# A decoder layer in one kernel: the feed-forward loop's fourth weight group joins the seven-product scheme, one weight sum of each group is made by a DMA

## The chip, the cores and the metric

One core of one Trainium2 chip. The time is the device time of one execution in microseconds (us); the kernel before takes 2042.21 us (median of three runs, 2042.13 to 2042.24).

## What is computed

A hybrid decoder layer on 256 tokens, model width 2048, float32 in and out:

```python
x = x + 0.5 * swiglu(rmsnorm(x, ffn1_norm), ffn1_w_gate, ffn1_w_up, ffn1_w_down)
h = rmsnorm(x, mix_norm)
merged = (sigmoid(g_d + b_gate_dil) * (dilated_attention(...) @ w_proj_dil)
          + sigmoid(g_f + b_gate_fox) * (forgetting_attention(...) @ w_proj_fox))
x = x + merged @ w_out
x = x + 0.5 * swiglu(rmsnorm(x, ffn2_norm), ffn2_w_gate, ffn2_w_up, ffn2_w_down)
return rmsnorm(x, final_norm)
# swiglu(x, g, u, d) = (silu(x @ g) * (x @ u)) @ d;  D_FF = 5632
```

The change touches the two `swiglu` stages only.

## The kernel before, in words

**Split products.** A float32 matrix is split into a rounded part (`..._hi`, type fp32r, made by ACT with a copy) and the rest (`..._lo`, made by DVE as original minus rounded). A product is three matmuls: hi·hi, hi·lo, lo·hi. Weights come in *loads* of 1 MB (four row blocks of 128 by 512 columns, tile `raw`, four places) and are used in *slabs* of two row blocks (128x1024 elements in a place). A slab goes through three engines: ACT rounds it (`round_step`, into `w_hi` or `more_hi`), DVE makes its low part (`split_step`, into `w_lo` or `more_lo`), PE multiplies. The slabs have a ring of six places (`FFN_RING`): ACT may round slab m only when PE has finished slab m-6, and each engine works its slabs in order. `hi_ready`, `lo_ready` and `slab_done` count them.

**A step of the feed-forward loop** (`ffn`, lines 946 to 978 for PE) makes one chunk of 512 of the 5632 hidden columns; a first chunk is made outside the loop (`FIRST`, 16 slabs), then come 10 steps (`STEPS`) in each of the two feed-forward stages, 20 in all. A step has 33 slabs. The 2048 rows of the gate and up weights are four groups of 512. Groups 1, 2 and 3 go by a scheme of Strassen's kind (`paired`): two token tiles and the two weights gate and up make a 2x2 block product with seven products in place of eight. Each of the seven is one slab on one token operand, 6 matmuls of 128x512. Three of the seven weight operands are plain halves of a load, the other four are sums T1 to T4 that DVE makes first (`weight_sum`, four additions of 128x1024 to a group, into tile `sums`). Group 0 is done directly: four slabs of 12 matmuls. Eight *down* slabs of 12 matmuls each, for the product of the chunk before with the down weight, end the step. DVE also turns the seven results into gate and up (`partial`, `up_sums`, `chunk_buf`: adds out of PSUM), makes `hidden`, and the low part of its transpose (`hT_lo`, 128x512 twice).

**What sets the order.** Every engine's order is written out in loops over the slab number o. ACT and DVE run six slabs ahead of PE: at o they handle slab o+6. The DVE line that places the sums (L1781 to L1786) puts T1 ahead of the split of the slab of its group with number 1, T2 ahead of number 2, T4 ahead of number 4, while the products stand in the order T3, gate, T1, T2, up, T4, gate (`PRODUCTS`, L112): every sum has at least one other slab's split between itself and its own slab's split. DVE's sequence of adds at the end is L1937 to L1971. SP issues each load when `lo_ready` has reached the slab given by `FREE` (L120). Down results are copied by ACT to `gate_buf` and added to `xres` by accumulating DMAs that POOL issues, four to a step (L1729 to L1735).

## Time and profile before

| | |
|---|---|
| median of three runs | 2042.21 us |
| span of the profiled execution | 2040.2 us |
| PE busy | 2027.8 us (99%), 9204 matmuls |
| DVE busy | 1858.9 us (91%) |
| ACT busy | 1267.5 us (62%) |
| POOL busy | 87.6 us (4%) |
| DMA | 441 MB, mean 216 GB/s |

The profiled execution has no time of its own beside its span (first to last instruction); the three runs, which lie within 0.11 us of each other, take 2.0 us more than that span. The span has the first feed-forward stage up to about 675 us, the attention and merge stages, and the second feed-forward stage from about 1360 us. Busy times of successive instructions of one engine overlap a little, so what an instruction costs its engine is read as the distance from its start to the next start. In a row of a timeline, an instruction's start, its duration, engine and line come first, then what it writes and reads; idle time before it and who ended that stand in brackets.

### The profile page before, as it was taken

The page shows a single profiled execution, that of the slowest core. Times are in us where ns is not written, and L with a number is a line of the kernel's source. Part 1 is how long each engine was busy: PE and PEld are TensorE (multiplying, and loading weights), DVE is VectorE, ACT ScalarE, POOL GpSimd, SP SyncE. Part 2 cuts the span into 40 slices and gives each one's busy share as a digit, 9 for nine tenths or more (in the row PEclk, how much of TensorE's full clock was granted, in tenths as well). Part 3 has the DMA queues.
Part 4 walks back from the last instruction along what each step waited for, and adds up shares of the span by engine and source line. Part 5 has one row for each costly group of instructions (what it writes and reads, how often), then busy time and mean ns, then how long its engine had stood idle before and what let it go on. Part 6 is the DMA issues. An engine that isn't in the chain of part 4 may idle for free.

```text
span 2040.2 us, 26364 instructions
## 1 busy us (share of the span) xinstructions
PE 2027.8 (99%) x9204; PEld 1678.7 (82%) x9204; DVE 1858.9 (91%) x1897; ACT 1267.5 (62%) x1474; POOL 87.6 (4%) x80
## 2 busy tenths in 40 slices
PE   9999999999999999999999999999999999999998
PEld 7888888888888888888888888888888888888886
DVE  7999999999999798887689999799999999999997
...
GB/s 301 206 211 259 230 236 246 227 236 227 246 247 235 157 186 183 198 177 157 183 134 227 189 243 182 211 186 192 242 223 250 244 232 211 260 225 240 247 231 127
DMA packets 222143, 441.03 MB, mean 216 GB/s; under 512 B 7648, under 2 KB 7824, under 8 KB 221936
## 3 DMA queue, kind: packets, MB, share of 16 engines
...
q8 instruction: 47, 0.77, 0.1%
...
HBM read 400.13 MB, written 2.10 MB: 197 GB/s over the span
## 4 chain that ended last, share of the span: by engine, by line
PE 98%; DVE 1%; ACT 0%; DMA 0%; issue 0%; SPq 0%; ACTq 0%; DVEq 0%
PE ps L765 16%; PE ps L767 16%; PE ps L766 16%; PE ps L778 12%; PE ps L780 12%; PE ps L779 12%; PE ps L1002 2%; PE ps L1003 2%; PE ps L1001 2%; PE ps L1050 2%; PE ps L1052 2%; PE ps L1051 2%; PE ps L856 1%; PE ps L834 0%; DMA xres<-in_x 0%; PE ps L1169 0%
## 5 line engine op out<-in xcount | busy, mean ns | idle before, releaser
L1788 DVE TENSOR_TENSOR w_lo<-raw,w_hi 128x1024 fp32r<-128x1024 f32 x280 | 337.9, 1219 | 7.2 <-ACT w_hi L1356 4.9
L1356 ACT ACTIVATE w_hi<-raw 128x1024 fp32r<-128x1024 f32 x280 | 290.8, 1053 | 72.6 <-PE ps L767 54.0
L1356 ACT ACTIVATE w_hi<-sums 128x1024 fp32r<-128x1024 f32 x160 | 169.8, 1063 | 204.8 <-PE ps L767 71.4
L1788 DVE TENSOR_TENSOR w_lo<-sums,w_hi 128x1024 fp32r<-128x1024 f32 x160 | 195.3, 1222 | 33.8 <-ACT w_hi L1356 31.1
L765 PE MATMUL ps<-w_hi,hT_hi 128*128 128x512 f32 x536 | 208.8, 390 | 0.0
L767 PE MATMUL ps<-w_hi,hT_lo 128*128 128x512 f32 x536 | 208.5, 389 | 0.0
L766 PE MATMUL ps<-w_lo,hT_hi 128*128 128x512 f32 x536 | 208.5, 389 | 0.0
L1788 DVE TENSOR_TENSOR more_lo<-raw,more_hi 128x1024 fp32r<-128x1024 f32 x140 | 169.2, 1219 | 6.6 <-ACT more_hi L1356 5.6
L765 PE MATMUL ps<-w_hi,xT_hi 128*128 128x512 f32 x424 | 170.1, 401 | 0.0
L1356 ACT ACTIVATE more_hi<-raw 128x1024 fp32r<-128x1024 f32 x140 | 146.4, 1054 | 32.6 <-PE ps L767 23.8
L767 PE MATMUL ps<-w_hi,xT_lo 128*128 128x512 f32 x424 | 165.7, 391 | 0.0
L766 PE MATMUL ps<-w_lo,xT_hi 128*128 128x512 f32 x424 | 165.2, 390 | 0.0
L1734 POOL DMA_DIRECT2D xres<-gate_buf x72 | 84.9, 1179 | 1848.3 <-ACT gate_buf L1490 1803.3
L1356 ACT ACTIVATE more_hi<-sums 128x1024 fp32r<-128x1024 f32 x80 | 85.1, 1063 | 99.1 <-DVE sums L1770 24.1
L778 PE MATMUL ps<-w_hi,xT_hi 128*128 128x512 f32 x354 | 139.8, 395 | 0.0
L780 PE MATMUL ps<-w_hi,xT_lo 128*128 128x512 f32 x354 | 138.1, 390 | 0.0
L779 PE MATMUL ps<-w_lo,xT_hi 128*128 128x512 f32 x354 | 137.9, 390 | 0.0
L1675 ACT ACTIVATE w_hi<-raw 128x1024 fp32r<-128x1024 f32 x87 | 92.2, 1060 | 63.6 <-PE ps L767 51.8
L2128 DVE TENSOR_TENSOR w_lo<-raw,w_hi 128x1024 fp32r<-128x1024 f32 x85 | 102.2, 1220 | 20.2 <-ACT w_hi L1576 20.2
L1576 ACT ACTIVATE w_hi<-raw 128x1024 fp32r<-128x1024 f32 x85 | 89.1, 1057 | 47.2 <-PE ps L1052 31.0
L2317 DVE TENSOR_TENSOR w_lo<-raw,w_hi 128x1024 fp32r<-128x1024 f32 x87 | 104.8, 1220 | 14.9 <-ACT w_hi L1675 14.9
L767 PEld LDWEIGHTS ps<-w_hi,hT_lo 128*128 128x128 f32 x536 | 100.6, 188 | 20.9
...
## 6 DMA issues: line engine op xcount, KB each, us to landing
...
```

The lines of the kernel that those rows point to most:

```text
L765: nc.tensor.matmul(acc, hi, hi_w[:, j], start=first and j == 0, stop=False)
L766: nc.tensor.matmul(acc, hi, lo_w[:, j], start=False, stop=False)
L767: done = nc.tensor.matmul(acc, lo, hi_w[:, j], start=False, stop=last and j == 1)
L778: nc.tensor.matmul(acc, hi, hi_w[:, j], start=first and j == 0, stop=False)
L779: nc.tensor.matmul(acc, hi, lo_w[:, j], start=False, stop=False)
L780: done = nc.tensor.matmul(acc, lo, hi_w[:, j], start=False, stop=last and j == 1)
L1356: nc.scalar.activation(slot_hi(place, offset), src, ACT.Copy).then_inc(hi_ready, 1)
L1576: nc.scalar.activation(slot_hi(place, r), src, ACT.Copy).then_inc(hi_ready, 1)
L1675: nc.scalar.activation(slot_hi(place, offset), src, ACT.Copy).then_inc(hi_ready, 1)
L1788: nc.vector.tensor_tensor(slot_lo(place, offset), step_source(r)[0], slot_hi(place, offset).bitcast(F32), ALU.subtract).then_inc(lo_ready, 1)
L2128: nc.vector.tensor_tensor(slot_lo(place, r), dil_source(e)[0], slot_hi(place, r).bitcast(F32), ALU.subtract).then_inc(lo_ready, 1)
L2317: nc.vector.tensor_tensor(slot_lo(place, offset), merge_source(offset)[0], slot_hi(place, offset).bitcast(F32), ALU.subtract).then_inc(lo_ ...
```

## The change

Group 0 becomes a fourth group of seven products (now `PAIR_AT` = 0, 7, 14, 21; the direct slabs go), so a step has 36 slabs: 28 of 6 matmuls and 8 of 12. The signs are arranged so that all weight sums are additions. T1 is no longer made by DVE but by a DMA that POOL issues, which adds the gate load's half onto the up load's half in `raw` (`add_t1`, 512 KB); it waits for T3's sum (which reads the same half) and for the gate load. The seven products have the order T3, gate, T2, up, T1, T4, gate (`FFN_PRODUCTS`). DVE places T2 ahead of the split of number 2 of its group, T4 ahead of number 3, and T3 of the *next* group ahead of number 4. The eight down slabs' low parts are made in four pieces of 128x2048. The second up bank goes, so one combining add shrinks from 128x1024 to 128x512; the adds follow the splits at o = 23 to 28. The fourth group's sums of tokens are made once per stage (`sum_pairs`, `split_pairs` with `PAIR_FOURTH`) and kept in places of `xT_hi`, `xT_lo` that are no longer read. The loads come in the order of the groups.

```diff
-FIRST, STEP = 2 * WIDE, 33
+FIRST, STEP = 2 * WIDE, 36
...
-PAIR_AT, PAIR_GROUPS, PAIR_SLABS = (0, 7, 18), (1, 2, 3), 7
-PAIRS = len(PAIR_AT)
-DIRECT_AT, DIRECT_GROUP = 14, 0
+PAIR_AT, PAIR_GROUPS, PAIR_SLABS = (0, 7, 14, 21), (1, 2, 3, 0), 7
+PAIRS, PAIR_FOURTH = len(PAIR_AT), 3
...
+FFN_PRODUCTS = (("sum", T3), ("gate", 0), ("sum", T2), ("up", 1), ("sum", T1), ("sum", T4), ("gate", 1))
+FFN_SUMS = (T3, T2, T4)
+FFN_PLACE = {T3: 0, T2: 0, T4: 1}
+SUMS_STEP = len(FFN_SUMS) * PAIRS
 SUMS = SUMS_STEP * STEPS
 
-PAIR_LOADS, DIRECT_LOADS, DOWN_LOADS = ((0, 1), (2, 3), (6, 7)), (4, 5), 8
-
-FREE = (-6, -4, -2, 0, 5, 7, 12, 14, 16, 18, 23, 25)
+PAIR_LOADS, DOWN_LOADS = ((0, 1), (2, 3), (4, 5), (6, 7)), 8
+
+FREE = (-6, -4, -2, 0, 5, 7, 12, 14, 19, 21, 26, 28)
...
+    F_M1, F_M6, F_M7, F_TURN, F_GATE, F_UP0, F_M5 = 0, 1, 2, 3, 4, 6, 7
...
+                    if pair == PAIR_FOURTH:
+                        return lambda j: of_x(CT * s + 2 * j, 1)
                     return lambda j: (pair_hi[:, s, 2 * pair + j], pair_lo[:, s, 2 * pair + j])
 
                 for o, (bank, lhs) in enumerate((
-                        (M7, of_pair(S3)), (M1, of_tile(0, 0)), (M5, of_pair(S1)), (M6, of_pair(S2)),
-                        (UP0, of_pair(S4)), (GATE + 1, of_tile(1, 1)), (GATE, of_tile(1, 0)))):
+                        (F_M7, of_pair(S3)), (F_M1, of_tile(0, 0)), (F_M6, of_pair(S2)), (F_UP0, of_pair(S4)),
+                        (F_M5, of_pair(S1)), (F_GATE + 1, of_tile(1, 1)), (F_GATE, of_tile(1, 0)))):
...
-                    for o in range(2):
-                        slab(place, DIRECT_AT + o, (GATE, GATE + 1), of_x, CT * DIRECT_GROUP + 2 * o,
-                             False, False)
-                    pe.wait_ge(ht_lo, hid + TT)
-                    for o in range(2):
-                        direct_up(place, DIRECT_AT + 2 + o, CT * DIRECT_GROUP + 2 * o, o == 0, o == 1)
...
+                    pe.wait_ge(s_lo, (f + 1) * PAIRS)
+                    for o in paired(place, PAIR_FOURTH):
+                        pass
+                    pe.wait_ge(ht_lo, hid + TT)
                     for n in range(NN):
 
-                        pe.wait_ge(combined, merged + (1, 3, 4, 5)[n])
+                        pe.wait_ge(combined, merged + (1, 2, 4, 5)[n])
...
-            def round_step(place, offset, count):
+            def round_step(place, offset, count, added_before):
 
                 q, r = divmod(offset, STEP)
                 kind, pair, o = step_slab(r)
                 src, l = step_source(r)
-                if l is None:
-                    act.wait_ge(summed, count + SUMS_STEP * q + 4 * pair + PRODUCTS[o][1] + 1)
+                if l is not None:
+                    act.wait_ge(raw_landed[l % LOADS], place.landed(STEP_LOADS * q + l))
+                elif FFN_PRODUCTS[o][1] == T1:
+                    act.wait_ge(t1_added[pair], (added_before + q + 1) * 16)
                 else:
-                    act.wait_ge(raw_landed[l % LOADS], place.landed(STEP_LOADS * q + l))
+                    at = FFN_SUMS.index(FFN_PRODUCTS[o][1])
+                    act.wait_ge(summed, count + SUMS_STEP * q + len(FFN_SUMS) * pair + at + 1)
...
+                    if o == FIRST - 1:
+                        act.wait_ge(slab_done, first.slab(FIRST))
+                        round_pairs(f, PAIR_FOURTH)
...
+            def add_t1(f, q, pair):
+
+                up_l, gate_l = PAIR_LOADS[pair]
+                place = step_place(f, q)
+                pool.wait_ge(summed, f * SUMS + q * SUMS_STEP + len(FFN_SUMS) * pair + 1)
+                pool.wait_ge(raw_landed[gate_l % LOADS], place.landed(gate_l))
+                pool.dma_start(raw[:, up_l % LOADS, 0::2, :], raw[:, gate_l % LOADS, 0::2, :],
+                               accum_op=ALU.add).then_inc(t1_added[pair], 16)
+
...
+            for f in range(2):
+                add_t1(f, 0, 0)
+                add_t1(f, 0, 1)
+                for q in range(STEPS):
+                    add_t1(f, q, 2)
+                    add_t1(f, q, 3)
+                    if q < STEPS - 1:
+                        add_t1(f, q + 1, 0)
+                        for n in range(3):
+                            add_down(f, q, n)
+                        add_t1(f, q + 1, 1)
+                        add_down(f, q, 3)
...
-                done = count + SUMS_STEP * q + 4 * pair
-                out = sums[:, SUM_PLACE[which]]
+                done = count + SUMS_STEP * q + len(FFN_SUMS) * pair
+                out = sums[:, FFN_PLACE[which]]
                 if which == T3:
-                    dve.wait_ge(lo_ready, place.slab(base + at - 2))
+                    dve.wait_ge(summed, done)
                     dve.wait_ge(raw_landed[up_l % LOADS], place.landed(STEP_LOADS * q + up_l))
-                    made = nc.vector.tensor_tensor(out, up[:, 1::2, :], up[:, 0::2, :], ALU.subtract)
-                if which == T1:
-                    dve.wait_ge(lo_ready, place.slab(base + at - 1))
-                    dve.wait_ge(raw_landed[gate_l % LOADS], place.landed(STEP_LOADS * q + gate_l))
-                    made = nc.vector.tensor_tensor(out, up[:, 0::2, :], gate[:, 0::2, :], ALU.subtract)
+                    made = nc.vector.tensor_tensor(out, up[:, 1::2, :], up[:, 0::2, :], ALU.add)
                 if which == T2:
                     dve.wait_ge(lo_ready, place.slab(base + at + 1))
-                    dve.wait_ge(summed, done + T3 + 1)
-                    made = nc.vector.tensor_tensor(out, sums[:, SUM_PLACE[T3]], gate[:, 0::2, :], ALU.add)
+                    dve.wait_ge(raw_landed[gate_l % LOADS], place.landed(STEP_LOADS * q + gate_l))
+                    made = nc.vector.tensor_tensor(out, sums[:, FFN_PLACE[T3]], gate[:, 0::2, :], ALU.add)
                 if which == T4:
-                    dve.wait_ge(lo_ready, place.slab(base + at + 3))
-                    dve.wait_ge(summed, done + T2 + 1)
-                    made = nc.vector.tensor_tensor(out, gate[:, 1::2, :], sums[:, SUM_PLACE[T2]], ALU.subtract)
+                    dve.wait_ge(lo_ready, place.slab(base + at - 1))
+                    dve.wait_ge(summed, done + 2)
+                    made = nc.vector.tensor_tensor(out, gate[:, 1::2, :], sums[:, FFN_PLACE[T2]], ALU.add)
                 made.then_inc(summed, 1)
 
             def split_step(place, offset, count, final=False):
 
                 q, r = divmod(offset, STEP)
                 kind, pair, o = step_slab(r)
-                if kind == "paired" and o in (1, 2, 4):
-                    weight_sum(place, q, pair, {1: T1, 2: T2, 4: T4}[o], count)
-                if r + 1 in PAIR_AT:
-                    weight_sum(place, q, PAIR_AT.index(r + 1), T3, count)
-                if r == STEP - 1 and not final:
+                if kind == "paired" and o == 2:
+                    weight_sum(place, q, pair, T2, count)
+                if kind == "paired" and o == 3:
+                    weight_sum(place, q, pair, T4, count)
+                if kind == "paired" and o == 4 and pair + 1 < PAIRS:
+                    weight_sum(place, q, pair + 1, T3, count)
+                if r == STEP - 2 and not final:
                     weight_sum(place, q + 1, 0, T3, count)
+                if kind == "down" and o % 2 == 0:
+                    return
                 dve.wait_ge(hi_ready, place.slab(offset + 1))
+                if kind == "down":
+                    hi, lo = slots(place, offset - 1)
+                    nc.vector.tensor_tensor(lo, raw[:, step_source(r)[1] % LOADS], hi.bitcast(F32),
+                                            ALU.subtract).then_inc(lo_ready, 2)
+                    return
                 nc.vector.tensor_tensor(slot_lo(place, offset), step_source(r)[0],
                                         slot_hi(place, offset).bitcast(F32), ALU.subtract).then_inc(lo_ready, 1)
...
+                    if o == WIDE + 4:
+                        sum_pairs(f, PAIR_FOURTH)
+                    if o == FIRST - 1:
+                        split_pairs(f, PAIR_FOURTH)
...
-                        if o == 22:
-                            dve.wait_ge(slab_done, place.slab(22))
-                            dve.wait_ge(m1_copied, i + (f * STEPS + 1))
-                            nc.vector.tensor_tensor(u2, ps[:, M6], partial[:, PART_M1],
-                                                    ALU.add).then_inc(combined, 1)
-                        if last and o == 25:
+                        if last and o == 28:
                             gate_sum(place)
-                        if last and o == 26:
+                        if last and o == 29:
                             dve.wait_ge(combined, merged + 4)
-                            multiply_up([up_sums[:, 1 - t] for t in range(TT)], i * TT + (silu + TT))
+                            multiply_up([up_sums[:, 1 - t] for t in range(TT)], i * TT + (silu + TT), rstd_q)
                         if not last or o + FFN_RING < STEP:
                             split_step(place, o + FFN_RING, i * SUMS_STEP + count, last)
                         else:
                             split_slab(last_place(f), o + FFN_RING - STEP)
                         if o == 6:
-                            split_tokens(hid, 0, T)
-                        if o == 11:
-                            split_tokens(hid, 1, T)
-                        if o == 22:
+                            split_tokens(hid, 0, F_TURN)
+                        if o == 13:
+                            split_tokens(hid, 1, F_TURN)
+                        if o == 23:
+                            dve.wait_ge(slab_done, place.slab(24))
+                            dve.wait_ge(m1_copied, i + (f * STEPS + 1))
+                            nc.vector.tensor_tensor(u2, ps[:, F_M6], partial[:, PART_M1],
+                                                    ALU.add).then_inc(combined, 1)
+                        if o == 24:
                             dve.wait_ge(combined, merged + 1)
-                            nc.vector.tensor_tensor(u3, ps[:, M7], u2, ALU.add).then_inc(combined, 1)
-                        if o == 23:
+                            nc.vector.tensor_tensor(u3, ps[:, F_M7], u2, ALU.add).then_inc(combined, 1)
+                        if o == 25:
+                            dve.wait_ge(slab_done, place.slab(25))
                             dve.wait_ge(combined, merged + 2)
+                            nc.vector.tensor_tensor(u2, ps[:, F_UP0], u2, ALU.add).then_inc(combined, 1)
+                        if o == 26:
+                            dve.wait_ge(slab_done, place.slab(26))
+                            dve.wait_ge(combined, merged + 3)
                             nc.vector.tensor_tensor(up_sums[:, :, :],
-                                                    ps[:, M5:M5 + 1].broadcast_to([P, TT, CH]),
+                                                    ps[:, F_M5:F_M5 + 1].broadcast_to([P, TT, CH]),
                                                     partial[:, PART_U3:PART_U2 + 1], ALU.add)\
                               .then_inc(combined, 1)
...
-                        if not last and o == 26:
+                        if not last and o == 28:
                             gate_sum(place)
-                        if not last and o == 28:
+                        if not last and o == 31:
                             dve.wait_ge(combined, merged + 4)
-                            multiply_up([up_sums[:, 1 - t] for t in range(TT)], i * TT + (silu + TT))
+                            multiply_up([up_sums[:, 1 - t] for t in range(TT)], i * TT + (silu + TT), rstd_q)
```

DVE's rows of the second last step (written out behind the loop, so that nothing stands between the operations), kernel before: T1's sum (L1766), T2's (L1770) and T4's (L1774) of the third group; L1788 is the split into the low part.

```order
L1766 TENSOR_TENSOR sums<-raw 128x1024 [waits raw_landed3,lo_ready]
L1788 TENSOR_TENSOR more_lo<-raw,more_hi 128x1024 [waits hi_ready]
L1770 TENSOR_TENSOR sums<-sums,raw 128x1024 [waits summed,lo_ready]
L1788 TENSOR_TENSOR w_lo<-sums,w_hi 128x1024 [waits hi_ready] x2
L1774 TENSOR_TENSOR sums<-raw,sums 128x1024 [waits summed,lo_ready]
L1788 TENSOR_TENSOR w_lo<-raw,w_hi 128x1024 [waits hi_ready]
L1788 TENSOR_TENSOR w_lo<-sums,w_hi 128x1024 [waits hi_ready]
```

After the change, second group of the second last step: T3's split, then T2's sum (L1795), T4's (L1799), and T3's of the third group (L1791); L1822 is the split.

```order
L1822 TENSOR_TENSOR more_lo<-sums,more_hi 128x1024 [waits hi_ready]
L1822 TENSOR_TENSOR w_lo<-raw,w_hi 128x1024 [waits hi_ready]
L1795 TENSOR_TENSOR sums<-sums,raw 128x1024 [waits raw_landed3,lo_ready]
L1822 TENSOR_TENSOR w_lo<-sums,w_hi 128x1024 [waits hi_ready]
L1799 TENSOR_TENSOR sums<-raw,sums 128x1024 [waits summed,lo_ready]
L1822 TENSOR_TENSOR w_lo<-raw,w_hi 128x1024 [waits hi_ready]
L1791 TENSOR_TENSOR sums<-raw 128x1024 [waits raw_landed0,summed]
L1822 TENSOR_TENSOR w_lo<-raw,w_hi 128x1024 [waits hi_ready]
L1822 TENSOR_TENSOR more_lo<-sums,more_hi 128x1024 [waits hi_ready]
```

Before, T2's sum had the splits of T1 and T2 behind it (the row with x2); now T2's own split is the next operation.

DVE at the end of that step after the change, from the last paired slab: L1819 splits two down slabs at once, L2004 to L2016 are combining adds.

```order
L1822 TENSOR_TENSOR w_lo<-raw,w_hi 128x1024 [waits hi_ready]
L1819 TENSOR_TENSOR w_lo<-raw,w_hi 128x2048 [waits hi_ready]
L2004 TENSOR_TENSOR partial<-ps,partial 128x512 [waits m1_copied,slab_done]
L2008 TENSOR_TENSOR partial<-ps,partial 128x512 [waits combined]
L1819 TENSOR_TENSOR more_lo<-raw,more_hi 128x2048 [waits hi_ready]
L2012 TENSOR_TENSOR partial<-ps,partial 128x512 [waits combined,slab_done]
L2016 TENSOR_TENSOR up_sums<-ps,partial 128x1024 [waits combined,slab_done]
L1819 TENSOR_TENSOR w_lo<-raw,w_hi 128x2048 [waits hi_ready]
L1791 TENSOR_TENSOR sums<-raw 128x1024 [waits raw_landed0,summed]
```

PE's first down product waits (`combined`) for the add of L2004, which stands behind the piece that holds slabs 28 and 29.

POOL in the loop, after the change (before, L1734 four times a step alone):

```order
L1741 DMA raw<-raw 128x2x512 [waits raw_landed1,summed]
L1741 DMA raw<-raw 128x2x512 [waits raw_landed3,summed]
L1741 DMA raw<-raw 128x2x512 [waits raw_landed1,summed]
L1750 DMA xres<-gate_buf 128x2x512 [waits down_added0,down_copied]
L1750 DMA xres<-gate_buf 128x2x512 [waits down_added1,down_copied]
L1750 DMA xres<-gate_buf 128x2x512 [waits down_added2,down_copied]
L1741 DMA raw<-raw 128x2x512 [waits raw_landed3,summed]
L1750 DMA xres<-gate_buf 128x2x512 [waits down_added3,down_copied]
```

The four new DMAs (L1741) share POOL's queue with the four old ones (L1750), in this fixed order.

## Rows read from the trace of the kernel before

**Rows 1.** Page of the kernel before: span, engines' busy time, end chain by engine

```profile
span 2040.2 us, 26364 instructions
...
PE 2027.8 (99%) x9204; PEld 1678.7 (82%) x9204; DVE 1858.9 (91%) x1897; ACT 1267.5 (62%) x1474; POOL 87.6 (4%) x80
...
PE 98%; DVE 1%; ACT 0%; DMA 0%; issue 0%; SPq 0%; ACTq 0%; DVEq 0%
```

**Rows 2.** Windows: the start, one step of the first loop, one of the second

```profile
core 0: us, PE busy (x) PEld busy (x) DVE busy (x) ACT busy (x) POOL busy (x), PEclk, DMA share, GB/s
0.00:10.00 10.00, 6.39 (x36) 5.52 (x37) 3.07 (x6) 3.42 (x5) 0.20 (x4) 1.00 0.72 261
305.92:368.09 62.17, 62.17 (x280) 51.47 (x279) 59.14 (x55) 40.13 (x43) 4.71 (x4) 1.00 0.77 236
1600.00:1662.17 62.17, 62.17 (x280) 51.47 (x279) 59.14 (x55) 40.15 (x43) 4.71 (x4) 1.00 0.77 236
```

**Rows 3.** Timeline of PE: end of one step, the next one up to its transposes

```profile
start us, us, engine line op out<-in xcount [idle before <-releaser]
...
304.40 0.39 PE L767 MATMUL ps<-w_hi,hT_lo 128*128 128x512 f32 x1
304.63 0.39 PE L778 MATMUL ps<-more_hi,pair_hi 128*128 128x512 f32 x1
...
311.20 0.39 PE L780 MATMUL ps<-w_hi,pair_lo 128*128 128x512 f32 x1
```

**Rows 4.** Timeline of ACT: last down slabs, then the step's first roundings

```profile
304.83 1.06 ACT L1356 ACTIVATE w_hi<-sums 128x1024 fp32r<-128x1024 f32 x1 [1.66 <-PE ps L767]
305.80 1.01 ACT L1490 ACTIVATE gate_buf<-ps 128x1024 f32<-128x1024 f32 x1
306.70 1.05 ACT L1356 ACTIVATE more_hi<-raw 128x1024 fp32r<-128x1024 f32 x1
...
314.23 1.06 ACT L1356 ACTIVATE w_hi<-sums 128x1024 fp32r<-128x1024 f32 x1 [1.21 <-DVE sums L1770]
```

**Rows 5.** Timeline of DVE in the same stretch

```profile
305.92 1.23 DVE L1788 TENSOR_TENSOR w_lo<-sums,w_hi 128x1024 fp32r<-128x1024 f32 x1 [1.49 <-ACT w_hi L1356]
307.07 1.22 DVE L1762 TENSOR_TENSOR sums<-raw 128x1024 f32<-128x1024 f32 x1
...
312.90 1.22 DVE L1770 TENSOR_TENSOR sums<-sums,raw 128x1024 f32<-128x1024 f32 x1
314.04 2.52 DVE L1788 TENSOR_TENSOR w_lo<-sums,w_hi 128x1024 fp32r<-128x1024 f32 x2
316.47 1.22 DVE L1774 TENSOR_TENSOR sums<-raw,sums 128x1024 f32<-128x1024 f32 x1
```

**Rows 6.** Timeline of DVE between third product group and down slabs

```profile
343.46 0.69 DVE L1942 TENSOR_TENSOR partial<-ps,partial 128x512 f32<-128x512 f32 x1
344.06 1.22 DVE L1788 TENSOR_TENSOR w_lo<-raw,w_hi 128x1024 fp32r<-128x1024 f32 x1
345.20 0.68 DVE L1959 TENSOR_TENSOR partial<-ps,partial 128x512 f32<-128x512 f32 x1
...
358.45 1.41 DVE L1866 SCALAR_TENSOR_TENSOR hidden<-up_sums,rstd,chunk_buf 128x512 f32<-128x512 f32 x2
359.78 1.22 DVE L1770 TENSOR_TENSOR sums<-sums,raw 128x1024 f32<-128x1024 f32 x1
```

**Rows 7.** DMA queues in that step (kind: packets, MB, share of 16 engines)

```profile
q1 hardware_dynamic: 6336, 12.58, 56.8%
q0 software_dynamic: 1089, 2.10, 20.4%
```

**Rows 8.** Tile xres over the whole span: POOL issue, and landing of its DMAs

```profile
L1734 POOL DMA_DIRECT2D xres<-gate_buf x72: 1168/1179/1222, 104.4 to 1949.6; - x72
...
DMA to landing us min/median/max: 4.7/5.5/10.4
```

**Rows 9.** Timeline of POOL: one of the four issues of the step

```profile
307.10 1.18 POOL L1734 DMA_DIRECT2D xres<-gate_buf  x1 [4.25 <-ACT gate_buf L1490]
```

146 lines of the change are left out of this document (72 added, 74 removed).

## The prediction

> **What bounds the kernel now.** I read the page first, then one step of the loop by windows, then the timelines of PE, ACT and DVE at the same stretch, and last the DMA queues. The page says that PE is busy 99% of 2040.2 us and that 98% of the chain that ended last lies on it, with DVE at 91% [rows 1]. A step takes 62.17 us in both stages, PE busy all of it at a granted clock of 1.00 (the level of 2.4 GHz), DVE busy 59.14 [rows 2]. Matmuls follow each other at (311.20 - 304.63)/29 = 0.2266 us, though each lasts 0.39 [rows 3]; 270 of them are 61.2 us, so the eight transposes cost the other 0.96. PE is the bound, and DVE is close behind it. The reader should see how close. DVE's 128x1024 operations last 1.22 but start 1.14 apart (312.90 to 314.04, 344.06 to 345.20; the readings are rounded to 0.01, and I take 1.135), 128x512 ones 0.60 apart (343.46 to 344.06), the two that make `hidden` 1.33 together [rows 5, 6]. A step has 33 splits, 12 sums and 3 combining adds of 1024, and 4 operations of 512: 48 x 1.135 + 4 x 0.60 + 1.33 = 58.2 us of densely packed work in 62.17. The four microseconds left are waits for the ring of six, such as the 1.49 at 305.92, where DVE waits for ACT and ACT for PE [rows 4, 5].
>
> **The change, part by part.**
>
> PE: six matmuls fewer a step (264 for 270), 6 x 0.2266 = 1.36 us. Were PE still the bound, a step would take 60.81 and 20 steps would save 27 us.
>
> DVE's work: 28 splits, 12 sums and two adds of 1024 make 42 x 1.135 = 47.67. The four splits of 2048 are not in the trace. From 512 to 1024 the distance grows by 0.535, so I take 1.135 + 2 x 0.535 = 2.205 each, 8.82 together; the ends would be 2 x 1.135 = 2.27 (nothing gained by merging) and 2.13 (no fixed part left). Five operations of 512 are 3.0, `hidden` 1.33. Sum 60.8: DVE alone is as long as PE alone, with no slack left.
>
> DVE's new gap: T2's sum is now directly followed by the split of the same slab, and that split needs ACT's rounding of the sum. The trace has each leg. T2's sum starts at 312.90, ACT's rounding at 314.23, for 1.06 [rows 4, 5]; the split of T2 is the second of the pair that begins at 314.04 and ends at 316.56, so it starts at 315.33. From sum to own split are 2.43 us, in which DVE did one other split. Now nothing stands between, so DVE is idle for 2.43 - 1.135 = 1.29, four times a step, 5.2 us. Nothing can cover it: DVE works in order. DVE's own cycle becomes 60.8 + 5.2 + some 0.3 for adds that wait for the add before them, 66.3 us.
>
> The path from one step's end on PE to the next: DVE can't work ahead without limit, since ACT rounds slab m only when PE has done slab m-6. I follow the step round. Slabs 0 to 27 are the paired ones, 28 to 35 the down ones.
> - PE's last down matmul ends at 304.79 (304.40 + 0.39). ACT rounds slab 5 (304.83), copies the last down bank (305.80) and rounds slab 6 until 307.75 [rows 3, 4]. T3's sum of the second group has moved ahead of slab 4's split, so DVE stands at slab 6 and starts it at 307.79: 3.00 us.
> - DVE then does 22 splits (slabs 6 to 27) and 8 sums: 30 x 1.135 = 34.05; three gaps behind T2, 3.87; two `hT_lo` of 512, 1.20.
> - The split of slabs 28 and 29 together, 2.21, since PE can start slab 28 only with the whole piece.
> - The first combining add, for which PE's first down product waits, 0.69 [rows 6], and 0.05 to PE.
> - PE's 96 down matmuls, 95 x 0.2266 + 0.39 = 21.92.
> The sum is 67.0 us. Between the two (down slabs' splits, the other adds, T3's sum, slabs 0 to 5) DVE has 0.7 us over, because its own cycle is 66.3.
>
> So a step goes from 62.17 to 67.0, +4.83. I take it for all 20 steps, 96.6 us: the first one of a stage too starts with at most six slabs ahead. There DVE splits the fourth group's token sums ahead of slab 6, 3.7 in place of 3.0 us, +0.7 twice, 1.4 us. The fourth group's sums themselves stand in the first chunk, where PE needs 12 matmuls, 2.72 us, to a slab and DVE 1.135: nothing.
>
> The DMAs: T1's sum leaves DVE, but it goes to POOL's queue and the same DMA engines. In the step, 12 loads take 56.8% of 62.17 us, 2.94 each, and four adds 20.4%, 3.17 each [rows 7]. Four more make 12 x 2.94 + 8 x 3.17 = 60.6 us of all engines in 67.0, 91% for 77% [rows 2]. A new add is issued when T3's sum is done, and ACT needs it before T1's split. Between them DVE does ten operations and a gap, 12.6 us; less the rounding, 11.4 remain, against a landing of 5.5 in the middle and 10.4 at most [rows 8]. On POOL the issue takes 1.18, and queued ahead of it can be a down add that waits for ACT's copy; the copies come 5.44 us apart (two down slabs of 12 matmuls), and T1 of the next step's first group, queued ahead of three of them, waits for its T3's sum, some 8 us behind the start of the down slabs. ACT needs the first down add only for the third copy, some 16 us in. I cost the DMAs at nothing; the cover is those 11.4 us. If it goes, each microsecond by which a T1 comes late stands on DVE's path, since the 0.7 us over is soon used up.
>
> Loads: `FREE` lets the first load of the next step go when the piece of slabs 28 and 29 is done; T3's sum needs it two pieces and three adds later, 2 x 2.2 + 2 x 0.6 + 0.6 + 1.135, 7.4 us. Likewise nothing, with 2 us to spare over 5.5.
>
> **Sum.** 2040.2 + 96.6 + 1.4 = 2138.2 us of span; the runs lie 2.0 us above the span, so **2140 us**, 4.8% slower.
>
> **Rivals.**
>
> The DMAs come late. For it speaks that the engines are at 91% on the mean and that T1 of the first two groups is due when the down adds run; against it, that landings in the trace hardly pass 7 us. With T1 late by 1 to 3 us once a step: 20 to 60 us more, 2160 to 2200. The Trainium skill (DMA: Bandwidth & Descriptors, "Issuing engines are not separate DMA queues") says that DMAs of all issuing engines run on the same 16 and interleave; by that the sum moved off DVE is not free, and the trace agrees, with 3.17 us of all engines for an add.
>
> The gap is not on the path: ACT is quick enough or something covers it, and only the DVE work counts. Then a step is 67.0 - 3 x 1.29 = 63.1, +1.0 us, and the time 2063. Against it speak the rows of both engines: ACT can't round before the sum ends.
>
> The other side: PE stays the bound and gets all of its saving, a step of 60.81, in all 2042.2 - 27.2 = 2015. This is so if the ring's lead of six slabs carries DVE over the 28 paired slabs; it decides by whether the chain above is under 60.8 us. It would have to be 6.2 shorter, more than all gaps in it (3.87), the late add (0.7) and ACT's copy (0.9) together. What could do it is only a 2048 split far cheaper than its size.
>
> POOL against DVE: if POOL's issue held up DVE, four more issues of 1.18 would add up to 4.7 us a step, 94 in all, 2234. Against it: POOL issued from 307.10 to 308.28, and DVE's sum from 307.07, with two inputs in SBUF, took 1.22 as ever [rows 5, 9]. The Trainium skill (SBUF — State Buffer, "SBUF: two separate sides") makes this a lock between a DVE operation with two SBUF inputs and a GpSimd one that reads SBUF; by that lock 2234 would come out, and these rows don't show it.
>
> PE's clock: it will now idle 9% in bits of up to 2 us. At the start it was busy 6.39 of 10 us at a clock of 1.00 [rows 2]. No case of its own.
>
> **How the numbers follow.** The chain as summed, 0.66: its own range is 2126 to 2156 (the 2048 split's ends, 0.1 us on the path; waits of 0.15 us that I leave out, some three to a step; a late DMA now and then). Late DMAs 0.20, gap off the path 0.06, PE the bound 0.05, POOL's lock 0.03. The range of 2118 to 2172 takes in the first and the nearer part of the second. About 0.2% (4 us) is what a measurement can tell from no change: faster 0.05, same 0.02, slower 0.93.
>
> **What would show it.** DVE: four idle times of about 1.3 us a step, in front of the low part of a sum, ended by ACT, whose own wait was for the T2 sum. PE: idle ahead of paired slabs, ended by DVE's `w_lo` and `more_lo`, about 6.2 us a step, most in the last two groups and ahead of the first down slab; steps 67.0 apart. The 2048 split 2.29 us long. ACT without waits for the DMA of `raw`. Wrong would be steps under 64, a DVE that waits mostly for PE's ring, or waits for T1's DMA of over 1 us a step.

## The result, and the profile after

The changed kernel takes **2203.84 us** (median of four runs, 2197.59 to 2211.25) against 2042.17 us for the kernel before: ratio 1.0792, 95% interval 1.0768 to 1.0816. The prediction had 2140 us and a range of 2118 to 2172: the direction is right, the size is outside the range by 32 us. The profiled execution has a span of 2204.3 us. Its four runs scatter by 14 us; the four of before lie within 0.2 us.

The page of the changed kernel, the lines that answer to [rows 1], the DMA queues, the groups that matter and the DMA issues:

```profile
PE 2059.9 (93%) x9084; PEld 1647.2 (75%) x9084; DVE 1915.4 (87%) x1889; ACT 1309.8 (59%) x1536; POOL 183.0 (8%) x160
...
q1 hardware_dynamic: 202112, 401.64, 52.7%
q0 software_dynamic: 41504, 80.23, 22.0%
...
PE 43%; DVE 21%; DMA 17%; issue 14%; ACT 5%; DVEq 0%; POOL 0%; ACTq 0%; SPq 0%; POOLq 0%
...
L1358 ACT ACTIVATE w_hi<-sums 128x1024 fp32r<-128x1024 f32 x160 | 169.0, 1056 | 354.5 <-DVE sums L1795 311.4
...
L1822 DVE TENSOR_TENSOR w_lo<-sums,w_hi 128x1024 fp32r<-128x1024 f32 x160 | 195.4, 1221 | 95.4 <-ACT w_hi L1358 95.4
...
L1819 DVE TENSOR_TENSOR w_lo<-raw,w_hi 128x2048 fp32r<-128x2048 f32 x60 | 136.9, 2281 | 0.5 <-ACT w_hi L1358 0.5
...
raw<-in_ffn_w_gate SPq DMA_DIRECT2D x87, 1024.0 KB, 8.1
...
raw<-raw POOLq DMA_DIRECT2D x80, 512.0 KB, 7.9
xres<-gate_buf POOLq DMA_DIRECT2D x72, 512.0 KB, 10.9
```

PE had 98% of the chain that ended last before and has 43% now (the line that begins with PE 43%); DVE has 21% and **DMA 17%**, which was no part of the forecast. The 2048 split lasts 2.28 us. DVE is idle 95.4 us in front of the low parts of sums in `w_lo`, always until ACT; 80 gaps of 1.21 us (the next rows) would be 97.

The gap behind T2, in the timeline of DVE in a step of the loop (the answer to [rows 5]): T2's sum (L1795), then nothing, then the split that needs ACT's rounding of that sum.

```profile
323.32 1.21 DVE L1795 TENSOR_TENSOR sums<-sums,raw 128x1024 f32<-128x1024 f32 x1
325.74 1.23 DVE L1822 TENSOR_TENSOR w_lo<-sums,w_hi 128x1024 fp32r<-128x1024 f32 x1 [1.21 <-ACT w_hi L1358]
326.88 1.22 DVE L1799 TENSOR_TENSOR sums<-raw,sums 128x1024 f32<-128x1024 f32 x1
```

From the start of the sum to the start of its split are 2.42 us (predicted 2.43), 1.21 of them idle after the end of the sum. Against a dense row of operations, which start 1.135 apart, that is 1.29 lost. It stands there four times a step.

The first combining add (L2004, [rows 6]) marks the steps. Its starts in the timeline of DVE:

```profile
172.86 0.68 DVE L2004 TENSOR_TENSOR partial<-ps,partial 128x512 f32<-128x512 f32 x1
...
240.16 0.68 DVE L2004 TENSOR_TENSOR partial<-ps,partial 128x512 f32<-128x512 f32 x1
...
307.68 0.68 DVE L2004 TENSOR_TENSOR partial<-ps,partial 128x512 f32<-128x512 f32 x1
...
377.98 0.68 DVE L2004 TENSOR_TENSOR partial<-ps,partial 128x512 f32<-128x512 f32 x1
...
450.83 0.68 DVE L2004 TENSOR_TENSOR partial<-ps,partial 128x512 f32<-128x512 f32 x1
```

The distances are 67.30, 67.52, 70.30 and 72.85. Five of the first stage's nine whole steps are 67.2 to 67.5 (67.0 predicted); the other four, and all nine of the second stage (70.4 to 73.0), are 3 to 6 us longer. The long step 307.68 to 377.98 shows why. First ACT's copies of the down banks and POOL's issues in it, and DVE behind them:

```profile
315.24 1.01 ACT L1495 ACTIVATE gate_buf<-ps 128x1024 f32<-128x1024 f32 x1
...
320.68 1.01 ACT L1495 ACTIVATE gate_buf<-ps 128x1024 f32<-128x1024 f32 x1
...
330.66 1.03 ACT L1495 ACTIVATE gate_buf<-ps 128x1024 f32<-128x1024 f32 x1 [4.00 <-DMA xres<-gate_buf]
```

```profile
317.96 1.18 POOL L1741 DMA_DIRECT2D raw<-raw  x1 [26.43 <-DMA raw<-in_ffn_w_gate]
318.67 1.68 POOL L1750 DMA_DIRECT2D xres<-gate_buf  x1
```

```profile
332.66 1.23 DVE L1822 TENSOR_TENSOR w_lo<-raw,w_hi 128x1024 fp32r<-128x1024 f32 x1 [2.29 <-ACT w_hi L1358]
```

The first copy is done at 316.25. Its down add stands in POOL's queue behind the next step's first T1, which waits for a gate load that SP issued at 311.31 and that lands at 317.96. So the down add is issued at 318.67, lands 12.0 us later, and only then may ACT overwrite its half of `gate_buf` with the third copy: ACT stands 4.00 us, and with it all roundings behind the copy. DVE loses 2.29 us by it (last row), and 0.45 and 0.23 at two more splits of this step, 2.97 of the 3.1 us by which the step is longer than 67.22. The second of the two follows a wait of 2.85 us of ACT for the next group's T1, whose add POOL had issued right behind the third down add. In all, the waits for transfers of the changed kernel (engine, tile and line, what it waited for: us, times, longest; the chain of waits by groups):

```profile
ACT gate_buf L1495 <- DMA xres<-gate_buf: 63.3, 20, 6.5
...
ACT w_hi L1358 <- DMA raw<-in_ffn_w_down: 43.6, 31, 2.6
...
DVE sums L1791 <- DMA raw<-in_ffn_w_up: 18.6, 15, 2.5
...
ACT more_hi L1358 <- DMA raw<-raw: 16.0, 18, 3.4
```

Not each of these waits costs time. The one for down loads (43.6 us) is there with 38.8 us also in the run with T1's adds small, whose steps are hardly ever late.

And the time from issue to landing of T1's adds (L1741), of the down adds (L1750), and last that of the down adds in the kernel before (L1734):

```profile
DMA to landing us min/median/max: 5.6/7.9/11.9
```

```profile
DMA to landing us min/median/max: 5.1/10.9/14.3
```

```profile
DMA to landing us min/median/max: 5.2/5.5/9.0
```

**Where the 164.1 us of span come from**, by the starts of L2004 (L1942 before): 18 whole steps at 67.22 for 62.15 are 91.3; the first mark comes at 105.7 for 95.1 and the two stages' marks lie 781.4 apart for 772.1, 19.8 together; from the last mark to the end both take 54.2. The remaining 53 us is the sum of what the 18 steps take above 67.22: **the lateness of transfers**, as the experiments show.

TensorE's clock fell in some of these steps. In five of the 18 the granted clock has one stretch of some 3 us at 1.2 GHz, each right behind idle time of PE (busy 0.01 us from 1546 to 1548, then a granted clock of 0.58 and 0.57 from 1550 to 1554; busy 0.00 us from 2118 to 2120, then 0.58 and 0.56). The five take some 9 us of PE's time. The step shown above has none of them, and the late steps with one (70.4 to 73.0) are hardly longer than those without (70.3 to 72.9), so the clock follows the lateness and makes little of it here.

### The profile page after: what moved, and what is told of

The parts are those of the page before. It is cut to its first block, busy times and chain, and to the rows that moved or that the text cites. A ratio compares the mean times of both kernels' runs of the same rounds, so it can differ in the third digit from the quotient of the medians.

```text
span 2204.3 us, 26606 instructions
## 1 busy us (share of the span) xinstructions
PE 2059.9 (93%) x9084; PEld 1647.2 (75%) x9084; DVE 1915.4 (87%) x1889; ACT 1309.8 (59%) x1536; POOL 183.0 (8%) x160
## 4 chain that ended last, share of the span: by engine, by line
PE 43%; DVE 21%; DMA 17%; issue 14%; ACT 5%; DVEq 0%; POOL 0%; ACTq 0%; SPq 0%; POOLq 0%
PE ps L779 9%; PE ps L781 9%; PE ps L780 9%; DVE w_lo L1822 7%; DMA raw<-in_ffn_w_up 6%; DMA xres<-gate_buf 5%; DMA raw<-in_ffn_w_gate 4%; DVE more_lo L1822 4%; ACT w_hi L1358 4%; PE ps L792 3%; PE ps L794 2%; PE ps L793 2%; DVE sums L1795 2%; DVE sums L1799 2%; PE ps L1049 1%
## 5 line engine op out<-in xcount | busy, mean ns | idle before, releaser
L1358 ACT ACTIVATE w_hi<-raw 128x1024 fp32r<-128x1024 f32 x320 | 328.4, 1050 | 84.6 <-DMA raw<-in_ffn_w_down 43.6
L1822 DVE TENSOR_TENSOR w_lo<-sums,w_hi 128x1024 fp32r<-128x1024 f32 x160 | 195.4, 1221 | 95.4 <-ACT w_hi L1358 95.4
L1822 DVE TENSOR_TENSOR w_lo<-raw,w_hi 128x1024 fp32r<-128x1024 f32 x200 | 243.5, 1217 | 36.4 <-ACT w_hi L1358 36.4
L1741 POOL DMA_DIRECT2D raw<-raw x80 | 100.7, 1259 | 1752.7 <-DVE sums L1791 1021.1
L792 PE MATMUL ps<-w_hi,xT_hi 128*128 128x512 f32 x474 | 191.1, 403 | 28.8 <-DVE w_lo L1822 28.8
L792 PE MATMUL ps<-w_hi,pair_hi 128*128 128x512 f32 x360 | 151.8, 422 | 65.6 <-DVE w_lo L1822 65.5
L793 PE MATMUL ps<-w_lo,xT_hi 128*128 128x512 f32 x474 | 185.0, 390 | 0.0
L794 PE MATMUL ps<-w_hi,xT_lo 128*128 128x512 f32 x474 | 184.9, 390 | 0.0
L1822 DVE TENSOR_TENSOR more_lo<-raw,more_hi 128x1024 fp32r<-128x1024 f32 x120 | 144.6, 1218 | 11.2 <-ACT more_hi L1358 11.2
L794 PE MATMUL ps<-w_hi,pair_lo 128*128 128x512 f32 x360 | 142.6, 396 | 0.0
L793 PE MATMUL ps<-w_lo,pair_hi 128*128 128x512 f32 x360 | 142.3, 395 | 0.0
L779 PEld LDWEIGHTS ps<-w_hi,hT_hi 128*128 128x128 f32 x576 | 108.1, 188 | 42.1 <-DVE w_lo L1819 15.4
L1819 DVE TENSOR_TENSOR w_lo<-raw,w_hi 128x2048 fp32r<-128x2048 f32 x60 | 136.9, 2281 | 0.5 <-ACT w_hi L1358 0.5
L792 PE MATMUL ps<-more_hi,xT_hi 128*128 128x512 f32 x280 | 115.0, 411 | 12.8 <-DVE more_lo L1822 12.8
## 6 DMA issues: line engine op xcount, KB each, us to landing
xres<-gate_buf POOLq DMA_DIRECT2D x72, 512.0 KB, 10.9
```

What stands on the lines that cost most here:

```text
L779: nc.tensor.matmul(acc, hi, hi_w[:, j], start=first and j == 0, stop=False)
L792: nc.tensor.matmul(acc, hi, hi_w[:, j], start=first and j == 0, stop=False)
L793: nc.tensor.matmul(acc, hi, lo_w[:, j], start=False, stop=False)
L794: done = nc.tensor.matmul(acc, lo, hi_w[:, j], start=False, stop=last and j == 1)
L1358: nc.scalar.activation(slot_hi(place, offset), src, ACT.Copy).then_inc(hi_ready, 1)
L1741: pool.dma_start(raw[:, up_l % LOADS, 0::2, :], raw[:, gate_l % LOADS, 0::2, :], accum_op=ALU.add).then_inc(t1_added[pair], 16)
```

## The experiments

In a run that makes one DMA small, the rest of that sum is left out, and the waits and the order of issues stay. Two causes are on the table: DVE's gap with the chain of 67 us that it lengthens (theory one), and late DMAs, either by their bytes on 16 engines that are shared or by their place in POOL's queue. In each run below, "clean" is the shortest step that repeats, and "late" the sum of what the 18 whole steps take above it; both are read in the profiled execution.

**T2's sum one split earlier.**

```diff
-                if kind == "paired" and o == 2:
+                if kind == "paired" and o == 1:
                     weight_sum(place, q, pair, T2, count)
```

> The changed kernel with T2's sum one place earlier on DVE, ahead of the split of the group's number 1 instead of number 2. Theory 1 (the gap between T2's sum and its own split lies on the path): one split now covers all but 0.3 us of the 1.2 us gap, so three gaps on the path shrink by 0.9 each, 2.7 us a step, 54 in all: about 2150 us. Theory 2 (the DMAs bound the step, the gap only fills time in which DVE would wait anyway): less than 20 us gained, 2185 or more.

Measured: 2163.58 us (2157.67 to 2165.98), ratio 1.0589 (1.0567 to 1.0611). Clean steps are 64.2, so 3.0 us leave each (2.7 expected). But 68 us are late, for 53 in the change: steps grow up to 71.8 in the second stage. Waits for transfers in this run:

```profile
ACT gate_buf L1495 <- DMA xres<-gate_buf: 67.5, 18, 6.7
...
ACT more_hi L1358 <- DMA raw<-raw: 50.4, 25, 4.4
```

The gap is real: 3.0 us a step are 60 us in 20 steps, of which 40 are left in the time. The rest goes back into late steps. The time lies between the two theories, as both hold. Part of the 68 us can be the clock: 13 of the 18 steps have a stretch at 1.2 GHz behind an idle PE, together some 25 us of PE's time. How much of it counts was not separated.

**The first down add ahead of the next step's first T1 on POOL.**

```diff
-                        add_t1(f, q + 1, 0)
-                        for n in range(3):
+                        add_down(f, q, 0)
+                        add_t1(f, q + 1, 0)
+                        for n in (1, 2):
                             add_down(f, q, n)
```

> The changed kernel with one swap in POOL's queue: the add of the first down result is issued ahead of the next step's first T1 add, not behind it. Theory 1 (the order of the queue: the down add stands behind a DMA that waits for a gate load, lands late, and ACT's third copy waits for it): ACT's 63 us of waits for that add go, and DVE's waits at slab 4 behind them, 40 to 60 us: 2145 to 2165. Theory 2 (the DMA engines are too full whatever the order): the lateness moves to T1, under 15 us gained.

Measured: 2179.08 us (2171.94 to 2190.60), ratio 1.0674 (1.0625 to 1.0723). Clean still 67.2 to 67.3, late 27 for 53. ACT waits 13.2 us for `xres` where it waited 63.3, but now it waits 44.8 us for T1's adds (19.5 before this edit):

```profile
ACT w_hi L1358 <- DMA raw<-raw: 27.0, 14, 3.2
ACT more_hi L1358 <- DMA raw<-raw: 17.8, 19, 2.7
ACT gate_buf L1495 <- DMA xres<-gate_buf: 13.2, 13, 1.8
```

The place in the queue is half of the lateness. Neither theory's number is met: 25 us are gained, for 40 to 60 or under 15. The clock stays at 1.00 in all of these steps, so steps are late without it.

**T1's add with 32 of 512 columns.**

```diff
-                pool.dma_start(raw[:, up_l % LOADS, 0::2, :], raw[:, gate_l % LOADS, 0::2, :],
+                pool.dma_start(raw[:, up_l % LOADS, 0::2, 0:32], raw[:, gate_l % LOADS, 0::2, 0:32],
```

> The changed kernel with T1's add cut to 32 of its 512 columns (the rest of that sum is left out; waits and issue order stay). Theory 1 (the bytes of the new adds make loads and down adds late): steps fall to the 67.0 us of the prediction, 2140 us. Theory 2 (the place in POOL's queue alone makes the down add late): the waits stay, 2185 or more.

Measured: 2158.85 us (2157.29 to 2162.41), ratio 1.0577. Issue, queue and waits are all there, the bytes are not: 15 of 18 steps take 67.0 to 67.5, and 4 us are late. The time is 19 us above the 2140 of the first theory. In the profiled execution, 17 us above the forecast span, 8.6 of them stand at the first mark (105.5) and the distance of the stages (781.4), as in the change, 4.3 are clean steps of 67.22 for 67.0, and 4 are late. Without the bytes of T1's adds hardly a step is late. The down adds land in 7.9 us in the middle here, for 10.9 in the change.

**The down adds with 32 of 512 columns**, T1's adds whole (the same edit on `xres` and `gate_buf` in `add_down`).

> The changed kernel, whose down adds carry 32 of 512 columns only (so most of the down products' sum over the steps is left out); T1's adds are whole and POOL's order is the change's. The counterpart of e3_t1_small. Theory that the sum of bytes of both kinds of adds is what makes the transfers late: like e3_t1_small, 2159 us (2150 to 2168), steps of 67 to 67.5. Theory that T1's adds come late by themselves (their landing of 7.9 us in the middle, behind loads of 1 MB): 2180 us or more, with ACT waiting for the DMA of raw as long as before, 16 us and more. Theory that the down add is late by its own place in the queue, behind the T1 add that waits for a load: also 2180 us or more, with ACT's third copy waiting up to 6 us.

Measured: 2156.71 us (2155.26 to 2157.18), ratio 1.0559 (1.0541 to 1.0576); clean 67.2, 3 us late. That is the first theory's number (2150 to 2168). ACT waits for a T1 add once, 1.5 us, and the landing of T1's whole adds is 6.9 us in the middle for 7.9. Either kind made small cures both: at steps of 67 us neither makes them late by itself, the two together do. What is left is a wait by the place in the queue:

```profile
ACT gate_buf L1495 <- DMA xres<-gate_buf: 18.5, 9, 4.4
```

**T1's sum back on DVE** (in place behind T4's, no T1 add at all).

```diff
...
-                pool.dma_start(raw[:, up_l % LOADS, 0::2, :], raw[:, gate_l % LOADS, 0::2, :],
-                               accum_op=ALU.add).then_inc(t1_added[pair], 16)
...
                     weight_sum(place, q, pair, T4, count)
+                    up, gate = (raw[:, l % LOADS, 0::2, :] for l in PAIR_LOADS[pair])
+                    nc.vector.tensor_tensor(up, up, gate, ALU.add).then_inc(t1_added[pair], 1)
```

> The changed kernel with T1's sum made by DVE in place (128x1024, ahead of the split of number 3) and POOL's four new adds gone. DVE's own cycle becomes 66.3 + 4 x 1.135 = 70.8 us, the path 67.0 + 3 x 1.135 = 70.4: about 2042 + 20 x 8.7 = 2216 us, within 10 of it, if DVE's work and gaps are the bound without the DMAs. If the new adds cost more than DVE's four sums, it is clearly under the changed kernel's 2204.

Measured: 2236.33 us (2235.96 to 2236.77), ratio 1.0951. Steps are 71.0 to 71.4, 4.2 above the change's clean 67.2, for four more operations of DVE. It is 20 us above what was expected; the first mark at 110.7 and the stages' distance of 786.5 are 30 us above those of before, more than was allowed for. The spread of the runs is 0.8 us where the change has 14; the run with the down adds small, with T1's adds whole and hardly a step late, has 1.9, so the scatter comes with the lateness and not with the adds as such. With DVE so full, T1's sum on the DMAs, late as they are, still is worth 32 us against a fourth sum on DVE.

**Both edits of order together** (T2 earlier, down add first).

> T2's sum one split earlier, as in e1_t2_early, and the first down add ahead of the next step's first T1 on POOL, as in e2_down0_first, together. Places in POOL's queue theory: the two edits touch different waits and their gains add: e2 took 25 us from the change, so 2164 - 25 = 2139 us (2130 to 2150), and ACT's third down copy hardly waits. Full engines theory: 12 loads and 8 adds need 60.6 us of all 16 DMA engines in a step of 64.2, 94% for 90%, so the transfers stay late wherever they are queued: 2155 us or more, with waits for T1's adds and for loads in place of those for the down add.

Measured: **2118.33 us** (2115.84 to 2125.56), ratio 1.0383 (1.0363 to 1.0404), the fastest of the variants that make all of the sums. That is below both theories (2130 to 2150; 2155 or more). The gains do more than add: 86 us together, for 40 and 25 alone. Clean 64.2, late 22. Three steps have a stretch at the lower clock, for 13 with T2's edit alone, which may be part of the surplus. ACT waits 4.7 us for `xres`, but still 70 us in 32 waits for T1's adds. The windows row of one clean step (us; busy time and count of PE, PEld, DVE, ACT, POOL; clock, DMA share, GB/s):

```profile
296.80:361.10 64.30, 62.19 (x273) 49.90 (x272) 61.71 (x54) 42.50 (x45) 9.43 (x8) 1.00 0.93 261
```

The DMA engines are busy 93% of this step, and yet it is not late: a high share alone does not make a step late. The order of issues, by this run and the one of the down add, counts with it.

**T2 earlier, T1's add small.**

> T2's sum one split earlier, and T1's accumulating DMA carries 32 of its 512 columns only (so most of T1's sum is left out). Theory that the bytes of the T1 adds are all that made e1_t2_early's steps longer than 64.2 us: every step is 64.2, and the time is e3_t1_small's less 20 x 3.0 us, 2159 - 60 = 2099 us (2092 to 2106). Theory that a shorter step meets the next limit by itself (loads or down adds that come late as soon as the step is under 67 us): 2112 us or more, with steps of 65 and above.

Measured: 2111.69 us (2107.59 to 2115.40), ratio 1.0332. It stands where the second theory begins (2112), 6 us above the range of the first. Ten of the 18 steps are 63.9 to 64.9, the others 65.3 to 68.1, 23 us late in all, with the DMA engines at 80% in a clean step. The wait is the old one, by queue order:

```profile
ACT gate_buf L1495 <- DMA xres<-gate_buf: 43.5, 12, 5.3
```

**All three** (T2 earlier, down add first, T1's add small).

> T2's sum one split earlier, the first down add ahead of the next step's first T1, and T1's DMA with 32 of 512 columns (most of T1's sum left out): everything that made a transfer late so far is taken away at once, to see what is left. Account in two parts (T2's gap, 3.0 us a step, and lateness of transfers, some 55 us in the changed kernel): with both gone all steps are 64.2 us, and 2204 - 55 - 60 = 2089 us (2084 to 2098). Theory that a step of 64.2 us is itself too short for the 12 loads and 4 adds behind each other on the chain load, T1, rounding: 2105 us or more, as e6_t2_small.

Measured: 2096.14 us (2094.13 to 2096.80), ratio 1.0263 (1.0246 to 1.0280). All 18 steps are 63.9 to 65.3, some 4 us late, `xres` lands in 6.9 us in the middle. This is the number of the account in two parts (2084 to 2098). First mark 102.6 and stages 778.4 apart. With the gap cut and hardly anything late, 54 us of loss remain: 37 in the 18 steps, whose chain is 64.2 us where PE alone had 62.15, 14 at the two stage beginnings, and the rest late.

**The first down piece as two splits of 1024, the first combining add between them**, on top of the two edits of order, and on top of the small T1 add.

```diff
-                if kind == "down" and o % 2 == 0:
+                if kind == "down" and o % 2 == 0 and o > 0:
                     return
...
-                if kind == "down":
+                if kind == "down" and o > 1:
                     hi, lo = slots(place, offset - 1)
...
-                        if o == 23:
+                        if o == 22:
                             dve.wait_ge(slab_done, place.slab(24))
```

> e5_t2_down0, and the first piece of 2048 columns (down slabs 28 and 29) undone: two splits of 1024 again, with the first combining add between them. Path theory: PE can start slab 28 after a split of 1024 and the add, 1.14 + 0.69, and not after the split of 2048 and the add, 2.28 + 0.69: 1.14 us a step less on the path, 23 us in all, e5 less 20 to 25. Theory that the late DMAs set the step: e5 within 8 us, since what the path gives is waited for elsewhere.

> e3_t1_small (T1's DMA with 32 of 512 columns, most of T1's sum left out), and the first piece of 2048 columns (down slabs 28 and 29) undone into two splits, the first combining add between them: the test of e7_single28 where few transfers are late. Path theory of the prediction: PE's slab 28 starts 1.14 us earlier in every step, steps of 66.1 for 67.2, 2159 - 23 = 2136 us (2131 to 2142). Theory that the path goes elsewhere (DVE's own cycle, or the first combining add, for which the matmuls and ACT's copy are late as soon as it moves up): 2150 us or more.

Measured: 2121.57 us (2117.28 to 2127.30) for the first, the same within the scatter as without the edit (2118.33), as the theory of late DMAs had it; its shortest steps are 64.65. For the second 2150.57 us (2148.61 to 2154.05), 8 us less than without it, on the side of the theory that the path goes elsewhere (2150 or more); clean steps fall from 67.2 to 66.4, not to 66.1, and 12 us are late for 4. In a clean step of this second run (305.6 to 372.0) DVE waits for nothing but its four gaps:

```profile
DVE w_lo L1822 <- ACT w_hi L1358: 4.8, 4, 1.2
```

So 66.4 is DVE's own cycle, and the prediction had that at 66.3: the path of 67.2 was 0.8 above it, and an edit of the path can give no more. In the first run ACT waits for T1's adds 105 us in 49 waits, 51 of them in the row below, for 70 in 32 without the edit, and for `xres` 30 us for 4.7. So what the path could give is waited for elsewhere:

```profile
ACT w_hi L1358 <- DMA raw<-raw: 50.7, 25, 3.2
```

**T1's sum by POOL's own adder** in place of a DMA, on top of the two edits of order.

```diff
...
-                pool.dma_start(raw[:, up_l % LOADS, 0::2, :], raw[:, gate_l % LOADS, 0::2, :],
-                               accum_op=ALU.add).then_inc(t1_added[pair], 16)
+                up, gate = (raw[:, l % LOADS, 0::2, :] for l in (up_l, gate_l))
+                pool.tensor_tensor(up, up, gate, ALU.add).then_inc(t1_added[pair], 1)
```

> e5_t2_down0, and T1's sum is made by POOL's own tensor_tensor (128 x 1024, in place) and not by an accumulating DMA: the same sum, 4 transfers of all 16 engines fewer in a step. Theory of bytes: DMA load goes back to 4 adds a step, the down adds land in about 5.5 us again, steps are 64.2 and the time is 2100 us (2092 to 2112), if DVE is not held up by POOL. Theory of a lock between POOL and DVE (the rival of the prediction, there for the issue of a DMA): each POOL operation stops DVE for its own length, at least 1.2 us if POOL is as quick as DVE, so 80 x 1.2 = 96 us on top, 2196 us or more, and DVE operations beside it are longer than 1.22 us in the trace.

Measured: 2226.36 us (2225.43 to 2226.69), ratio 1.0900 (1.0881 to 1.0918), steps of 70.5 to 71.0, none late. It is 108 us above the same kernel with T1's DMA, on the side of the theory of a lock (2196 or more). POOL's group, then DVE and POOL at one of the four places, then the windows row of a step (columns as above):

```profile
L1742 POOL TENSOR_TENSOR raw<-raw 128x1024 f32<-128x1024 f32 x80 | 323.2, 4040 | 1198.5 <-DVE sums L1792 1189.2
```

```profile
359.67 3.28 POOL L1742 TENSOR_TENSOR raw<-raw 128x1024 f32<-128x1024 f32 x1 [5.89 <-DVE sums L1792]
```

```profile
359.49 1.22 DVE L1823 TENSOR_TENSOR w_lo<-raw,w_hi 128x1024 fp32r<-128x1024 f32 x1
360.63 3.40 DVE L1823 TENSOR_TENSOR more_lo<-sums,more_hi 128x1024 fp32r<-128x1024 f32 x1
363.95 0.68 DVE L1898 TENSOR_TENSOR hT_lo<-ps,hT_hi 128x512 fp32r<-128x512 f32 x1
```

```profile
321.90:392.80 70.90, 64.13 (x273) 49.46 (x272) 70.39 (x54) 42.16 (x45) 20.39 (x8) 1.00 0.70 206
```

A DVE operation beside POOL's lasts 3.40 us in place of 1.22: it ends at 364.03, 1.08 us after POOL's (362.95), as if it had begun only then. DVE's busy time in a step is 70.39 for 61.71, 2.2 us for each POOL addition. The two take turns and don't share. The Trainium skill (SBUF — State Buffer, "SBUF: two separate sides") tells of such a lock between a DVE operation with two SBUF inputs and a GpSimd one that reads SBUF; this trace agrees. In the change there is none of it beside POOL's *issues*: 186 DVE operations of 128x1024 run at the same time as one, and none is longer than 1.23 us.

**The kernel before with T1's sum by DMA alone**: order of products T3, gate, T2, up, T1, T4, gate; three T1 adds in a step; direct slabs, down splits and signs as before, so that T1 adds where it should subtract.

```diff
...
+FFN_PRODUCTS = (("sum", T3), ("gate", 0), ("sum", T2), ("up", 1), ("sum", T1), ("sum", T4), ("gate", 1))
...
-                if kind == "paired" and o in (1, 2, 4):
-                    weight_sum(place, q, pair, {1: T1, 2: T2, 4: T4}[o], count)
+                if kind == "paired" and o in (1, 3):
+                    weight_sum(place, q, pair, {1: T2, 3: T4}[o], count)
...
+                    if q < STEPS - 1:
+                        add_down(f, q, 0)
+                        add_t1(f, q + 1, 0)
+                        for n in (1, 2, 3):
+                            add_down(f, q, n)
+                        add_t1(f, q + 1, 1)
```

> The kernel before with one part of the change alone: T1's sum of its three pairs by an accumulating DMA, in the order of products that this needs (T3, gate, T2, up, T1, T4, gate), with the down add ahead of the next T1 on POOL; direct slabs, down splits of 1024 and signs as before, so that T1 adds where it should subtract (that part of the computation differs). PE has its 270 matmuls, DVE three sums less. Theory that the adds cost nothing while PE is the bound and DVE has slack: 2042 us (2038 to 2046). Theory that the transfers come late as soon as 12 loads and 7 adds, 12 x 2.94 + 7 x 3.17 = 57.5 us, must go through in 62.2 (92%): 2052 us or more, with ACT waiting for the DMA of raw or of xres and PE idle behind it.

Measured: 2099.88 us (2092.45 to 2112.05), ratio 1.0271 (1.0243 to 1.0299). It is on the side of the second theory (2052 or more). With PE as the bound and DVE relieved of three sums a step, this form of the adds costs 58 us. In the profiled execution, the slowest of the four, the steps are 63.1 to 70.7. Landing of the T1 adds, and the waits:

```profile
DMA to landing us min/median/max: 7.1/10.3/13.3
```

```profile
ACT w_hi L1365 <- DMA raw<-raw: 129.8, 32, 7.8
...
ACT more_hi L1365 <- DMA raw<-raw: 65.7, 20, 5.9
```

Two reserves keep this run from being the price of the adds alone. T3's sum stands one slab ahead of its group here and not three, and no gap stands behind T2: between T3's sum and T1's split DVE does seven operations and not ten and a gap, 7.9 us for the 12.6 of the prediction, and an add that lands in 10.3 us in the middle can hardly be in time. ACT waits 195 us for T1's adds, for 19.5 in the change. And nine steps have a stretch at the lower clock, some 20 us of PE's time, in a kernel that PE bounds. How much of the 58 us either makes was not tried.

## Why the prediction was right and wrong

Right, by its own steps. The **gap behind T2**: 1.21 us measured after the end of the sum, four times a step, and with the sum moved one split up the step falls by 3.0. **DVE's own cycle** of 66.3: 66.4 where the last run on the path laid it bare. The **2048 split**: it lasts 2.28 us, for 2.29 forecast. The **path** of 67.0: 67.2 in the clean steps. PE's saving of 27 us is worth nothing while this path is longer, as it said. POOL's issues do not hold up DVE, as it said; the lock that the rival spoke of exists for POOL's arithmetic.

Wrong: the step "I cost the DMAs at nothing; the cover is those 11.4 us". It put the wait for transfers at nothing, and the runs show 53 us of it. Of the 66 us by which the span is above the forecast (2204.3 for 2138.2), 53 are this, 9 stand at the stage beginnings and 4 are clean steps of 67.22 for 67.0. The step failed in four places.

- *The landing.* It set 5.5 us, the middle of a kernel with 77% on the DMA engines, against the cover at 91%. The adds land in 7.9 and 10.9 in the middle, up to 14.3. The 10.4 that it took from [rows 8] as the largest belongs to one of the four loads of x at the start, which that view of the tile takes in; the adds alone had 9.0 at most.
- *The victim.* It looked at T1 and gave the down adds one sentence: "ACT needs the first down add only for the third copy, some 16 us in". Counted from when that add can go, the room is far less: the copies are 5.44 apart, so from the end of the first (316.25) to the third's turn (326.66, where ACT began to wait) are 10.4 us. Of these POOL lost 2.4 behind T1's wait for a gate load; 8.0 remained for a landing of 12.0.
- *The start of T1's cover.* It counted from T3's sum. But T1's add also needs its gate load, and POOL waited 705 us in 36 waits for that, though many of those are idle time that cost nothing; behind such a wait stand the down adds.
- *The loads.* They were put at nothing too, "with 2 us to spare over 5.5". The up loads land in 6.6 us in the middle, and DVE's T3 sum waits for one 15 times, 18.6 us. With T1's adds small that wait is 0.3 us.

The rival "the DMAs come late" had 0.20 and 2160 to 2200, with T1 as what comes late; it was the case that came, through a down add first of all, and the time is 4 us above its far end. Its size, 1 to 3 us a step, was 2.9 on the mean (53 us in 18 steps). The range ended at 2172 and took in only its nearer part; a rival that rests on a shared resource at 91% should have had the range up to its far end.

A smaller miss: 4.83 us for each of the 20 steps and 1.4 for the token sums are 11.1 us at the two stage beginnings, where 19.8 were measured. From 40 us to the first mark of the first stage DVE has 64 operations with 60.0 us busy, where before had 57 with 53.8. The 6.2 more are a 2048 split (2.3) and the fourth group's token sums and their split (six operations, 4.1 us); the prediction had the sums at nothing and the split at 0.7. The idle time there, most of it the gaps behind T2, grows by 4.4. Together they are the 10.6 us of the first mark. A slip besides: its cover for the loads, 7.4 us, adds up to 7.3.

The second stage's steps are all late and half of the first stage's aren't, with the same instructions. Why stays open. The prediction gave the clock no case of its own; it fell in five steps, for some 9 us of PE's time.

No variant beats the kernel before. In the fastest of those built on the change hardly anything is late and T1's sum is mostly left out, and it still is 2.6% slower: the chain is 64.2 us, and PE's saving would need it under 62.15.
